# A separate transfer and split for the first k tile of the first weight tile, with 11 warming matmuls in place of 17

## The reference

```
h    = RMSNorm(x, norm_g)                  # x * rsqrt(mean(x^2)) * gain
proj = h @ w_in                            # 2048 -> 6400 columns: q, k, v, gates of two mixers
ya   = chunked attention, relative bias    # 16 heads of 64, times silu(gate)
yb   = sliding-window GQA, rotary, sinks   # 16 heads of 64, 2 kv heads, times silu(gate)
x    = x + concat(ya, yb) @ w_out          # 2048 -> 2048
```

## Time and profile before

| what | value |
|---|---|
| median of 3 runs | 1632.35 us (1632.01 to 1632.53) |
| profiled execution, its own time | 1632.42 us |
| profiled execution, first to last instruction (span) | 1630.5 us |
| PE busy | 1620.0 us (99% of the span) |
| DVE, ACT, POOL busy | 1050.8, 874.5, 94.1 us |
| HBM | read 159.58 MB, written 8.47 MB |

### The profile page before, as it was taken

How to read it: one execution, slowest core, us unless ns; L and a number is a source line. 1 busy time by engine, 2 the same in 40 slices (tenths; PEclk the granted TensorE clock), 3 DMA queues, 4 the chain that set the end, 5 groups by cost and what they waited for, 6 DMA issues and landing times.

```text
span 1630.5 us, 23794 instructions
## 1 busy us (share of the span) xinstructions
PE 1620.0 (99%) x8214; PEld 1375.7 (84%) x8214; DVE 1050.8 (64%) x2346; ACT 874.5 (54%) x1907; POOL 94.1 (6%) x74
## 2 busy tenths in 40 slices
PE   9999999999999999999999999999999999999997
PEld 8888888888888888899888888888888888888997
DVE  7555555555577777777755555555556677787765
ACT  7555655555546666333545555655546466654333
POOL 0000000000122200000000000000002212000000
PEclk9999999999999999999999999999999999999998
DMA  7232222231322322444432232222232323223343
GB/s 252 90 103 102 86 80 89 89 115 66 110 95 91 98 104 91 136 147 149 138 129 78 89 114 90 89 77 89 92 113 84 104 90 101 95 91 123 130 136 117
DMA packets 49725, 173.77 MB, mean 107 GB/s; under 512 B 6464, under 2 KB 10848, under 8 KB 35696
## 3 DMA queue, kind: packets, MB, share of 16 engines
q1 hardware_dynamic: 49184, 172.16, 31.5%
q10 hardware_dynamic: 432, 0.55, 0.1%
q0 software_dynamic: 32, 0.08, 0.0%
HBM read 159.58 MB, written 8.47 MB: 103 GB/s over the span
## 4 chain that ended last, share of the span: by engine, by line
PE 99%; DMA 0%; DVE 0%; ACT 0%; DVEq 0%; issue 0%; SPq 0%; ACTq 0%
PE ps_proj L580 23%; PE ps_proj L582 23%; PE ps_proj L581 23%; PE ps_o L642 2%; PE ps_t L632 2%; PE ps_o L794 1%; PE ps_o L798 1%; PE ps_o L799 1%; PE ps_s L624 1%; PE ps_s L623 1%; PE ps_proj L794 1%; PE ps_proj L798 1%; PE ps_proj L799 1%; PE ps_o L682 1%; PE ps_s L657 1%; PE ps_o L580 1%
## 5 line engine op out<-in xcount | busy, mean ns | idle before, releaser
L580 PE MATMUL ps_proj<-act_hi,w_hi 128*128 128x512 f32 x1632 | 645.4, 395 | 0.0
L582 PE MATMUL ps_proj<-act_hi,w_lo 128*128 128x512 f32 x1632 | 637.7, 391 | 0.0
L581 PE MATMUL ps_proj<-act_lo,w_hi 128*128 128x512 f32 x1632 | 636.3, 390 | 0.0
L1279 DVE TENSOR_TENSOR w_lo<-w_raw,w_hi 128x512 fp32r<-128x512 f32 (+1 forms) x528 | 380.8, 737 | 174.8 <-ACT w_hi L892 172.5
L892 ACT ACTIVATE w_hi<-w_raw 128x512 fp32r<-128x512 f32 (+1 forms) x528 | 331.0, 649 | 128.2 <-DVE w_raw L1578 61.7
L582 PEld LDWEIGHTS ps_proj<-act_hi,w_lo 128*128 128x128 f32 x1632 | 306.3, 188 | 66.6
L581 PEld LDWEIGHTS ps_proj<-act_lo,w_hi 128*128 128x128 f32 x1632 | 307.1, 188 | 57.3
L580 PEld LDWEIGHTS ps_proj<-act_hi,w_hi 128*128 128x128 f32 x1632 | 306.8, 188 | 56.8
L958 ACT ACTIVATE probs<-probs,nmax 128x128 f32<-128x128 f32 (+3 forms) x128 | 71.9, 562 | 111.1 <-DVE nmax L1342 108.8
L892 ACT ACTIVATE probs<-probs,rden 128x128 f32<-128x128 f32 (+3 forms) x128 | 72.1, 563 | 107.1 <-DVE rden L1363 107.1
L1279 DVE TENSOR_TENSOR arena<-ps_t,arena 128x512 fp32r<-128x512 f32 (+4 forms) x168 | 85.0, 509 | 44.8 <-ACT arena L892 43.8
(11 more groups left out here) (260 smaller groups left out, 2199.2 us busy)
## 6 DMA issues: line engine op xcount, KB each, us to landing
w_raw<-w SPq DMA_DIRECT2D x107, 1024.0 KB, 4.8
w_raw<-w SPq DMA_DIRECT2D x98, 256.0 KB, 3.7
temp<-temp SPq DMA_DIRECT2D x72, 64.0 KB, 4.1
strips<-ext SPq DMA_DIRECT2D x16, 256.0 KB, 5.7
temp<-xT SPq DMA_DIRECT2D x16, 256.0 KB, 4.1
xs<-xy SPq DMA_DIRECT2D x16, 256.0 KB, 3.4
temp<-xs SPq DMA_DIRECT2D x16, 256.0 KB, 2.7
strips<-ext SPq DMA_DIRECT2D x16, 224.0 KB, 5.8
```

What stands on the lines that cost most here:

```text
L580: pe.matmul(dst, wh, act_hi[:, k, :], start=start, stop=False)
L581: pe.matmul(dst, wh, act_lo[:, k, :], start=False, stop=False)
L582: return pe.matmul(dst, wl, act_hi[:, k, :], start=False, stop=stop)
L1279: return nc.vector.tensor_tensor(dst, src, hi, ALU.subtract)
```

## The change

Chunk 0 of weight tile 0 (four k tiles, 256 KB) is no longer one transfer and one split but two. ACT issues the first k tile's 128 columns (64 KB, rows of 512 B) with a semaphore of its own, `w_head`, and then the other three k tiles (192 KB, rows of 1536 B) with `w_first[0][0]`. ACT makes the high part of the first block, then that of x tile 0, then that of the other three blocks, then goes on with x tile 1; DVE does the low parts in the same order. PE's first k tile waits for `w_lo_head`, and its second for `w_lo_done`, which now counts the remainder. WARM falls from 17 to 11.

```diff
-WARM = 17
+WARM = 11
...
+        w_head = sem("w_head")
+        w_hi_head = sem("w_hi_head")
+        w_lo_head = sem("w_lo_head")
...
-            def project(T, s, pt, ready=None, ps=None, count=None, split=None):
+            def project(T, s, pt, ready=None, ps=None, count=None, split=None, head=False):
 
                 ps = ps_proj[s % 2] if ps is None else ps
                 for k in range(pt * KC, (pt + 1) * KC):
-                    if k % KC == 0:
+                    if head and k < 2:
+                        pe.wait_ge(*((w_lo_done, 1) if k else (w_lo_head, 1)))
+                    elif k % KC == 0:
                         if split is None:
                             pe.wait_ge(w_lo_done, T * PTS + (s * PTS + k // KC + 1))
...
-                            count=first_done if pt < PTS - 1 else None)
+                            count=first_done if pt < PTS - 1 else None, head=L == 0 and pt == 0)
...
-            for n in range(2):
-                act.dma_start(w_raw[:, n, chunk(0)], w[n][:, chunk(0)]).then_inc(w_first[n][0], 16)
+            for cols, landed in ((slice(0, P), w_head), (slice(P, KC * P), w_first[0][0])):
+                act.dma_start(w_raw[:, 0, cols], w[0][:, cols]).then_inc(landed, 16)
+            act.dma_start(w_raw[:, 1, chunk(0)], w[1][:, chunk(0)]).then_inc(w_first[1][0], 16)
...
                     if L < 1:
-                        split_first(0, c, 16)
+                        if c == 0:
+                            act.wait_ge(w_head, 16)
+                            copy(w_hi[:, 0, 0:P], w_raw[:, 0, 0:P]).then_inc(w_hi_head, 1)
+                        else:
+                            split_first(0, c, 16)
...
                         nc.scalar.activation(act_hi[:, k, :], xy[:, k, :], ACT.Copy,
                                              scale=gain_sb[:, bass.ds(L * KT + k, 1)]).then_inc(h_hi_done, 1)
+                        if L < 1 and k == 0:
+                            act.wait_ge(w_first[0][0], 16)
+                            copy(w_hi[:, 0, P:KC * P], w_raw[:, 0, P:KC * P]).then_inc(w_hi_done, 1)
...
-                    if L < 1:
+                    if L < 1 and c == 0:
+                        dve.wait_ge(w_hi_head, 1)
+                        low(w_lo[:, 0, 0:P], w_raw[:, 0, 0:P], w_hi[:, 0, 0:P].bitcast(F32)).then_inc(w_lo_head, 1)
+                    elif L < 1:
                         split_w(0, 0, c)
...
                             gain_sb[:, bass.ds(L * KT + k, 1)]).then_inc(h_lo_done, 1)
+                        if L < 1 and k == 0:
+                            dve.wait_ge(w_hi_done, 1)
+                            low(w_lo[:, 0, P:KC * P], w_raw[:, 0, P:KC * P], w_hi[:, 0, P:KC * P].bitcast(F32)
+                                ).then_inc(w_lo_done, 1)
```

## The result

The changed kernel takes 1634.68 us (median of 20 runs, 1632.1 to 1635.65) against 1632.37 (median of 20, 1631.98 to 1632.83): a ratio of 1.0013 (95% interval 1.0007 to 1.0019), so 2.3 us slower, and its runs spread over 3.5 us in place of 0.9. 17 of its 20 runs lie above 1633.3, none of the kernel before. The median lies outside the predicted range.

The account below looks back on a forecast made before the run. PE was taken to bound the kernel (99% of the wait chain). 1632.42 us profiled, less 0.2 for x tiles 2 and 3, plus 0 for head, splits, issue and warming, gave 1632.2, or 1632.15 as median; range 1631.6 to 1632.9.

Parts of the forecast that it names:

- The first product's start: On PE after the warming matmuls: first product at 6.4 us instead of 8.05.
- the head's landing: First 64 KB of chunk 0 on ACT's queue: lands at 4.6 us, between 4.24 and 5.70.
- the price of the splits: Weight split in two: 0.2 us more on ACT, 0.06 on DVE, covered before x tiles 2 and 3 land.
- ACT's later readiness: One more issue on ACT, 0.45 us, moves its readiness from 4.02 to about 4.47, hidden by its wait for weights.
- x tiles 2 and 3 might land sooner: Their 512 KB transfer, which holds the third k tile: 0.2 us earlier, between 0.6 earlier and 0.2 later.
- rival A: Alternating queue packets land x tiles 2 and 3 the full 0.6 us earlier: third k tile 9.3, total 1631.75; chance 0.16.
- the remainder lands about when the whole did: Chunk 0's other three k tiles: ACT's split of them starts from 5.8 us, the second k tile at 7.8.
- Rival C: Remainder or x tiles 2 and 3 late by 0.3 to 1 us, passed on by ACT's order: 1632.7 to 1633.4; chance 0.09.
- The prediction's own signs: Wrong altogether if the third k tile starts before 9.2 or after 10.3, or the total moves by other than that start.
- B: Idle PE loses its clock, half pace from the third k tile: 0.6 to 3.3 us or more; chance 0.04 within 0.2%, 0.02 beyond.
- The six warming matmuls: WARM from 17 to 11, 12 instructions fewer: PE free for products at 6.24 not 8.05, counted 0 in the sum.
- the sign chances: Chances for the total against a 0.2% bound (3.3 us): slower 0.02, within 0.97, faster 0.01.

Follow-up runs that it names:

- the two halves: Kernel before, with chunk 0 of weight tile 0 in two transfers of 64 partitions each, rows still 2 KB: 1633.39 us in one execution.
- all 17: Changed kernel with WARM back from 11 to 17, the transfer and split still in two: 1632.88 us (1632.2 to 1634.72).
- the one-transfer kernel: Changed kernel with chunk 0 in one transfer again, splits still in two and 11 warming matmuls: 1633.51 us (1632.62 to 1634.34).

## Why the prediction was wrong

**What held.** The first product's start (6.68, forecast 6.4), the head's landing (4.8, forecast 4.6), the price of the splits, ACT's later readiness: all within 0.3 us. That a faster head is worth nothing at the end, and that x tiles 2 and 3 might land sooner, held too: they came 1.3 us sooner, twice rival A's bound.

**The step that failed first** is a clause in brackets: "the remainder lands about when the whole did", 5.8. It landed at 7.95. I applied the turns of the two queues to x's transfer alone and not to the weights that pay for them; by the same reasoning the remainder had to be later by what x gained. Rival C had the place and the mechanism (late remainder, ACT's order passes it on) at up to 1 us and a chance of 0.09; it came to 2.15 in the transfer and to 1.0 at the third k tile. The prediction's own signs said so at once: a third k tile after 10.3 (it started at 10.92), and a total that moved by more than that start (2.2 us of span against 1.0 us). How much of the lateness is turns by rows and how much the added transfer stays open: the two halves show the second alone at work, the microsecond from 3.6 to 4.6 us the first.

**The step that failed worst** was to price B and C apart. The idle time before the third k tile was forecast at 1.3 us; C makes it 2 and more, and this is what B's condition hangs on. So B needed a chance close to C's, not 0.06. Against B I had set that the clock held near the end through 1.2 us of thin work and fell after 2.5, which reads a single fall as a limit. In the runs the same length had both outcomes: 2.52 us idle in the two halves and the clock stayed up, 2.49 with all 17 and it fell; 1.65 and it stayed, 1.64 and it fell. By these executions a hole gives a chance of losing the clock, and that is the likely source of most of the spread of 3.5 us.

**The step that looked safe.** The six warming matmuls stood at nothing in the sum, because they stood in the way of products. With them the late remainder cost 0.56 us in the median, without them 2.3. How they did it is not shown: in the one profiled execution with all 17 the wait was longer, 2.49 us, and the clock was lost all the same. That the kernel before owes its narrow spread to PE being at work from 1.37 us on almost without a gap fits all these runs, but only argument ties it to the single one.

By the bound of 0.2% the sign chances (0.97 for within) stand; the number and the range, 1631.6 to 1632.9, do not.

## What to carry to other kernels

A transfer cut in two so that its first part comes sooner pays with its second part, here by 1.5 to 2.9 us, and with it everything that an in-order engine has behind the wait for it; look for the landing of the *last* piece that the consumer needs. At the start of a kernel count PE's idle time by its effect on the clock, not only by its length: the holes of 1.5 to 2.5 us here cost more than a microsecond again in some executions and nothing in others. Warming work is therefore best measured by the spread of many runs, and matmuls of zeros in a hole that cannot be closed are a remedy (1.9 to 2.2 of 2.3 us here).

## What the hardware showed that I had not expected

- A place further back in an issuing queue costs even a small transfer microseconds while the other queue is loaded: 24 KB of gains issued second landed 5.2 us after their issue, where they had taken 3.0 as first, and in the two halves ACT's queue moved 2 packets in a microsecond between its first and its second transfer. Yet transfers on a queue do overlap: in the changed kernel ACT's queue had moved 0.42 MB by 7.5 us, so that some 0.13 MB of tile 1's chunk or more (the three transfers ahead of it are 0.29 MB) went before the remainder was whole at 7.95.
- Small rows in one queue hand the bandwidth to the other: from 3.6 to 4.6 us ACT's queue moved 0.20 MB in 106 packets before and 0.06 MB in 116 after.
- What one queue loses the other wins: x tiles 2 and 3 landed at 7.85 to 8.22 us with chunk 0 in one transfer, at 6.56 to 8.05 with two, at 6.55 with four.
- The rise of the clock is not tied to a count of matmuls: the same 34 warming instructions took 6.93 us in the kernel before and 5.45 in one execution of the kernel with all 17, the same 22 took 5.06 and 4.22.
- The clock column reads 1.00 up to the first recorded change, also where the matmuls' distance shows 1.2 GHz (0.43 us in the one-transfer kernel, whose window from 9 to 10 us reads as below). The distance of the starts decides.

```profile
9.00:10.00 1.00, 1.00 (x4) 1.00 0.99 356
```
